# A routing map scattered into a DRAM scratch in place of a stage of one-hot matmuls, in a fused decoder layer

## The reference

```python
def peer_ffn(xn, w_q, sub_keys, u, v):
    q = (t @ w_q).reshape(T, PEER_HEADS, 2, PEER_HALF)
    s = jnp.einsum('thpd,hpnd->thpn', q, sub_keys)
    s_top, i_top = lax.top_k(s, PEER_TOPK)                       # 16 of 128, on each of two sides
    cand_s = s_top[:, :, 0, :, None] + s_top[:, :, 1, None, :]   # 256 candidates
    cand_i = i_top[:, :, 0, :, None] * PEER_KEYS + i_top[:, :, 1, None, :]
    best_s, pos = lax.top_k(cand_s, PEER_TOPK)
    ids = take_along_axis(cand_i, pos)                           # 8 heads x 16 experts for each token
    gates = jax.nn.softmax(best_s, axis=-1)
    act = gelu(einsum('td,ted->te', x, u[ids]))
    y = einsum('te,ted->td', gates * act, v[ids])
```

## Time and profile before

| | |
|---|---|
| median of 3 runs | 1158.25 us (1155.82 to 1158.5) |
| profiled execution, first to last instruction (span) | 1152.3 us |
| PE busy | 1085.2 us, 94% of the span |
| DVE busy | 786.0 us, 68% |
| ACT busy | 621.2 us, 54% |
| POOL busy | 120.7 us, 10% |
| moved by DMA | 179.54 MB, mean 156 GB/s |
| granted TensorE clock, mean | 0.980 |

### The profile page before, as it was taken

One profiled execution on the slowest core, in us unless ns is written; L12 is line 12 of the kernel. 1 busy time (PEld: TensorE's weight loads), 2 busy tenths in 40 slices (PEclk: granted clock), 3 DMA queues, 4 the chain that ended last, 5 costly groups with the idle time before them and its releaser, 6 DMA issues.

```text
span 1152.3 us, 20363 instructions
## 1 busy us (share of the span) xinstructions
PE 1085.2 (94%) x7278; PEld 1002.3 (87%) x7278; DVE 786.0 (68%) x1333; ACT 621.2 (54%) x1034; POOL 120.7 (10%) x101
## 2 busy tenths in 40 slices
PE   7999999989999999999999976667999999999998
PEld 6988999889899999999999975656888888888886
DVE  5774674453488889888884489998555555555554
ACT  6775555453555555555555576665545545455453
POOL 0000110010000000000000067884000000000000
PEclk9999999999999999999999988898999999999999
DMA  9544345252355454555445520001555555555552
GB/s 318 167 149 145 111 167 163 74 183 110 112 181 184 180 184 180 182 184 182 183 180 185 185 86 0 0 0 36 188 204 191 185 198 200 182 191 207 184 187 105
DMA packets 60658, 179.54 MB, mean 156 GB/s; under 512 B 4048, under 2 KB 42960, under 8 KB 44112
## 3 DMA queue, kind: packets, MB, share of 16 engines
q1 hardware_dynamic: 60624, 179.09, 44.7%
HBM read 178.03 MB, written 1.05 MB: 155 GB/s over the span
## 4 chain that ended last, share of the span: by engine, by line
PE 48%; issue 40%; DVE 7%; ACT 2%; POOL 2%; DMA 1%; DVEq 0%; POOLq 0%; SPq 0%; ACTq 0%
PE acc L1262 30%; PE acc L1044 13%; PE bank L1243 2%; DVE act_w L968 2%; DVE oh_i L957 2%; DVE oh_j L957 1%; POOL oh_i L320 1%; ACT wsp L347 1%; DVE wsp L663 1%; DMA wraw<-w_in 1%; PE bank L1148 0%; PE bank L1126 0%; POOL sqd L327 0%; PE bank L1073 0%; POOL wsp L312 0%
## 5 line engine op out<-in xcount | busy, mean ns | idle before, releaser
L886 DVE TENSOR_TENSOR hl<-raw,hl 128x1024 fp32r<-128x1024 f32 x192 | 234.4, 1225 | 170.0 <-ACT hl L577 168.2
L577 ACT ACTIVATE hl<-raw 128x1024 fp32r<-128x1024 f32 x192 | 202.6, 1056 | 135.7 <-PE acc L1262 126.3
L1262 PE MATMUL acc<-hl,whl 128*128 128x512 f32 x1152 | 266.6, 389 | 1.8 <-DVE whl L985 1.8
L1262 PEld LDWEIGHTS acc<-hl,whl 128*128 128x128 f32 x1152 | 216.3, 188 | 46.6 <-issue 1.9
L1214 PE MATMUL bank<-xt,hl 128*128 128x256 f32 x768 | 218.1, 284 | 0.0
L1215 PE MATMUL bank<-xt,hl 128*128 128x256 f32 x768 | 217.5, 283 | 0.0
L1216 PE MATMUL bank<-xt,hl 128*128 128x256 f32 x768 | 217.5, 283 | 0.0
L1214 PEld LDWEIGHTS bank<-xt,hl 128*128 128x128 f32 x768 | 147.5, 192 | 0.3 <-DVE hl L886 0.3
L1215 PEld LDWEIGHTS bank<-xt,hl 128*128 128x128 f32 x768 | 147.6, 192 | 0.2 <-issue 0.2
L1216 PEld LDWEIGHTS bank<-xt,hl 128*128 128x128 f32 x768 | 147.5, 192 | 0.0
L663 DVE TENSOR_TENSOR wsp<-wraw,wsp 128x2048 fp32r<-128x2048 f32 x35 | 80.2, 2290 | 73.9 <-ACT wsp L347 73.7
(11 more groups left out here) (207 smaller groups left out, 1448.3 us busy)
## 6 DMA issues: line engine op xcount, KB each, us to landing
raw<-u_t SPq DMA_DIRECT2D x64, 1024.0 KB, 4.8
raw<-v SPq DMA_DIRECT2D x64, 1024.0 KB, 4.7
wraw<-w_in SPq DMA_DIRECT2D x9, 1024.0 KB, 8.0
wraw<-w_pq SPq DMA_DIRECT2D x8, 1024.0 KB, 5.2
wraw<-w_ck SPq DMA_DIRECT2D x4, 1024.0 KB, 5.0
wraw<-w_cv SPq DMA_DIRECT2D x4, 1024.0 KB, 4.9
wraw<-w_out SPq DMA_DIRECT2D x4, 1024.0 KB, 4.9
wraw<-w_cq SPq DMA_DIRECT2D x4, 1024.0 KB, 5.0
```

The source lines that it names most:

```text
L577: nc.scalar.activation(eslot(k, 0, second), raw[:, k // 2, k % 2], ACT.Copy).then_inc(ready, 1)
L886: V.tensor_tensor(eslot(k, 1, second), raw[:, k // 2, k % 2], eslot(k, 0, second).bitcast(F32), ALU.subtract).then_inc(ready, 1)
L1262: last = pe.matmul(acc[:, 2 * t + n], a, b[:, 512 * n:512 * n + 512], start=False, stop=last_key and k == 2, skip_group_check=True)
```

## The change

The routing stage is gone. In its place W stands as an array `wmap` of 128 x 128 x 256 floats (16.8 MB) in DRAM:
- SP fills it with zeros in 8 transfers of 2.1 MB between the weight units 10 to 24 (new L260), from a tile of zeros that POOL clears at the start.
- Each routing pass ends with 16 addresses for each of its 128 tokens (`widx`), and its gates are normalised by themselves, two and four keys later: ACT's Exp (new L618) and two small instructions of DVE (new L917, L918).
- POOL then issues 16 indirect transfers for the pass (new L342), each of which adds one float per token to `wmap`: 256 transfers of 128 floats in all. Before a pass it waits until the pass of the previous head on the same tokens has landed.
- When all have landed, SP loads `wmap` for two keys at a time (256 KB, new L277 and L285) behind each load of v, and POOL multiplies it into act_w (`weigh`, new L348), 64 times. ACT splits a key of act_w only after that.
- ACT's loop over the keys is written out, and PE no longer transposes krow.

```diff
@@ SP
             for u in range(WRAW, NU):
                 unit(u)
+                if u % 2 == 0 and u // 2 - U_CK // 2 in range(NZERO):
+                    z = (u - U_CK) // 2
+                    n = KEYS * T // 512 // NZERO
+                    sp.dma_start(wz[:, z * n:z * n + n], zeros[:].unsqueeze(1).broadcast_to([P, n, 512])).then_inc(s_zero, 16)
...
             for q in range(2):
                 sp.wait_ge(s_ul, KEYS - 4 + 2 * q + 2)
                 sp.dma_start(raw[:, q], vd[q]).then_inc(s_raw[q], 16)
+            for t in range(TT):
+                sp.wait_ge(s_sca[t], 16 * TOPK * PH)
+            for q in range(2):
+                sp.dma_start(wblk[:, q], wm[:, WBK * q:WBK * q + WBK]).then_inc(s_wb[q], 16)
             sp.wait_ge(s_um, KEYS)
             sp.dma_start(gfin[:], g_final.rearrange("(o d) -> o d", o=1).broadcast_to([P, D])).then_inc(s_gf, 16)
             with sp.Fori(1, KEYS // 4) as it:
                 for q in range(2):
                     sp.wait_ge(s_vl, it * 4 - 4 + 2 * q + 2)
                     sp.dma_start(raw[:, q], vd[ds(it * 2 + q, 1)].rearrange("o i j d -> (o i) j d")).then_inc(s_raw[q], 16)
+                    sp.wait_ge(s_A, it * 2 + q - 1)
+                    sp.dma_start(wblk[:, q], wm[:, ds(it * (2 * WBK) + WBK * q, WBK)]).then_inc(s_wb[q], 16)
@@ POOL
-            (gate_rows, differences and their loop)
+            pool.wait_ge(s_zero, 16 * NZERO)
+            for n in range(NPASS):
+                t, h = n % TT, n // TT
+                pool.wait_ge(s_gr, n + 1)
+                if h:
+                    pool.wait_ge(s_sca[t], 16 * TOPK * h)
+                for k in range(TOPK):
+                    nc.gpsimd.indirect_dma_start(
+                        out=wmap, out_offset=bass.IndirectOffsetOnAxis(ap=widx[:, n, k:k + 1], axis=0),
+                        in_=gate[:, n, k:k + 1], in_offset=None, compute_op=ALU.add).then_inc(s_sca[t], 16)
+            def weigh(b, q):
+                aw = act_w[:, ds(b * WBK, WBK)]
+                nc.gpsimd.tensor_tensor(aw, aw, wblk[:, q], ALU.mult).then_inc(s_A, 1)
+            for b in range(2):
+                pool.wait_ge(s_ua, WBK * b + WBK)
+                pool.wait_ge(s_wb[b], 16)
+                weigh(b, b)
+            pool.wait_ge(s_ua, KEYS)
+            with pool.Fori(1, NWB // 2) as it:
+                for q in range(2):
+                    pool.wait_ge(s_wb[q], it * 16 + 16)
+                    weigh(it * 2 + q, q)
@@ ACT
+                if exps < NPASS and j == pass_key(exps) + 2:
+                    g = gate[:, exps]
+                    act.wait_ge(s_rt, exps + 1)
+                    nc.scalar.activation(g, g, ACT.Exp, accum_out=stat[:, GS + exps:GS + exps + 1]).then_inc(s_ge, 1)
+                    exps += 1
...
             for k in range(4):
+                if k % WBK == 0:
+                    act.wait_ge(s_A, k // WBK + 1)
                 a_high(k, k)
@@ DVE
+                if normed < NPASS and j == pass_key(normed) + 4:
+                    gate_norm(normed)
+                    normed += 1
+                if parts < 4 * NPASS and j == part_key(parts):
+                    route_part(parts // 4, parts % 4)
...
-            (onehots, weigh and their loop)
```

More of the change, by code:

```diff
@@ L19 @@
 X = mybir.AxisListType.X
+XY = mybir.AxisListType.XY
 ds = bass.ds
@@ L55, with build @@
 DVE_EVAC = set(range(U_OUT, U_CV3)) | set(range(U_CO, U_PQ))
-JPB = 8
-GRP = 4
-def build(nc, x, mem, par, wa, wx, w, keys_t, u_t, v, g_final, out):
+NPASS = TT * PH
+NZERO = 8
+WBK = 2
+NWB = KEYS // WBK
+def build(nc, x, mem, par, wa, wx, w, keys_t, u_t, v, g_final, wmap, out):
     ctx = ExitStack()
@@ L293, in _ @@
             nc.gpsimd.memset(ones[:], 1.0).then_inc(s_const, 1)
+            for t in range(TT):
+                nc.gpsimd.iota(tcol[:, t:t + 1], pattern=[[1, 1]], base=P * t, channel_multiplier=1,
+                               allow_small_or_imprecise_dtypes=True).then_inc(s_const, 1)
             nc.gpsimd.memset(cx[:, :, 0:CONV - 1], 0.0).then_inc(s_const, 1)
@@ L585, in _ @@
                 split_high(k, 16 if k % 2 == 0 else None, (s_seed, 1) if k == 2 else None, s_uh)
[L586 to L607, removed]
@@ L610, in onehots @@
[L610 to L618, removed]
-                last.then_inc(s_sqd, 1)
-                act.wait_ge(s_sqd, n + 1)
-                nc.scalar.activation(oh_j(slot), sqd(slot), ACT.Relu, scale=-1.0, bias=ones[:, 0:1]).then_inc(s_oja, 1)
@@ L623, in _ @@
-            act.wait_ge(s_kte, 3)
-            for slot in range(3):
-                onehots(0, slot, slot, GRP * slot, slot, True)
-            with act.Fori(1, T // GRP // 4) as it:
-                for slot in range(3):
-                    onehots(it, it * 3 + slot, it * 4 + slot, it * (4 * GRP) + GRP * slot, slot, False)
+            exps = 0
+            for j in range(KEYS):
+                gelu(j, j)
+                n = (j + 4) // 2
+                if j < KEYS - 4:
+                    split_high(j % 4, 16 * (n // 2 + 1) if j % 2 == 0 else None, (s_um, j + 1), s_uh)
+                elif j < KEYS - 1:
+                    split_high(j % 4, 16 * (n // 2 + 1) if j % 2 == 0 else None, (s_um, j + 1), s_vh, second=True)
+                if exps < NPASS and j == pass_key(exps) + 2:
[3 more added lines that the diff above has]
+                    exps += 1
@@ L1216, in u_keys @@
                         last = pe.matmul(bank[k][:, 0:T], ul[:, c], xt[:, c, 0], start=False, stop=(c == DC - 1))
-                    if last_pass and k < 3:
-                        if k == 0:
-                            pe.wait_ge(s_gr, 1)
-                        for t in range(TT):
-                            last = pe.transpose(bank[k][:, T + P * t:T + P * t + P], krow[:, k, t], ident[:])
                     last.then_inc(s_um, 1)
             u_keys(0, first=True)
-            with pe.Fori(1, KEYS // 4 - 1) as it:
+            with pe.Fori(1, KEYS // 4) as it:
                 u_keys(it)
-            u_keys(KEYS // 4 - 1, last_pass=True)
-            pe.wait_ge(s_ua, KEYS)
-            pe.wait_ge(s_kte, 3)
-            def route(it, slot, first=False):
-                pe.wait_ge(s_gi, it * 4 + (slot + 1))
-                if slot == 3:
-                    pe.wait_ge(s_ojd, it + 1)
-                else:
-                    pe.wait_ge(s_oja, it * 3 + (slot + 1))
-                if not first:
-                    pe.wait_ge(s_gw, it * 4 + (slot - 3))
-                for k in range(GRP):
-                    last = pe.matmul(bank[slot][:, P * k:P * k + P], oh_i(slot)[:, k], oh_j(slot)[:, k], start=True, stop=True)
-                last.then_inc(s_gm, 1)
-            for slot in range(4):
-                route(0, slot, first=True)
-            with pe.Fori(1, T // GRP // 4) as it:
-                for slot in range(4):
-                    route(it, slot)
             def v_wait(j):
```

184 lines of the change are left out of this document (67 added, 117 removed).

## The result

| | before | after |
|---|---|---|
| median | 1158.38 us (4 runs, 1155.82 to 1159.26) | 1223.61 us (4 runs, 1221.51 to 1224.97) |
| ratio after / before | | 1.0567 [1.0551, 1.0583] |
| span of the profiled execution | 1152.3 us | 1222.3 us |
| granted TensorE clock, mean | 0.980 | 0.912 |

The change makes the kernel 5.7% slower. The forecast was 1066 us, on the other side of no change. The time lies inside the range. The spans differ by more than the medians do, 70.0 us against 65.2. In every other run the time is 2.0 us above its span, as in 1224.35 and 1222.3 here, so the profiled execution of before was one of some 1154.3 us, about 4 us quicker than the median of its kernel.

The account below looks back on a forecast made before the run. PE was taken to bound the key and value stages, DVE the routing stage between. Span 1152.3 - 95.8 + 4 = 1060.5 us, plus 5.95 for the median, gave 1066 us; range 1034 to 1250.

Parts of the forecast that it names:

- What bounds the kernel, what goes: Key and value stages bound by PE, routing by DVE; removing routing starts the value stage at 673.8, gaining 124.4 us.
- The later of 673.8 and 344.0 + 256 X: Start of the value stage: everything else ready at 673.8, or POOL's 256 transfers plus a 6.6 us tail.
- the term X: Time POOL takes for each of 256 indirect transfers, chosen as 1.4 us; value start 702.4, gain 95.8 us.
- the 1.77 from which nothing is left: Time per POOL transfer, in us, at which the value stage starts at 798.2 as before, leaving no gain.
- the rival in which POOL is held until the landing: POOL waits for each transfer to land, 2.1 us each: value start 881.6, time 1246 us; chance 0.27.
- the forecast's own range: Whole kernel with 1.0 to 1.7 us per transfer and small losses: 1034 to 1144 us; chance 0.50.
- DVE's hold: Rival: DVE's two-input operations hold up POOL's transfers, 0.45 us each; value start 817.6, time 1182 us; chance 0.08.
- The start of 856 us: Value stage start if POOL were held for the skill's 2.0 us fixed per transfer: slower by 58 us.
- The DMA engines as the bound: Rival: small additions delay loads of u, the key stage grows by 54 us, time 1092 us; chance 0.06.
- a cost of the zeros: Filling the map between weight units 10 and 24: 2 us taken, up to 34 us if writes ran at half speed.
- The small losses: Zeros 2 us, Exp 0, DVE's key stage 0, key-stage traffic 1 us, value stage 1 us: 4 us in all.
- three signs of being wrong: Transfer spacing outside 1.0 to 1.7 us, PE waiting inside the key stage, ACT's value-stage waits naming POOL.

Follow-up runs that it names:

- experiment 3: The changed kernel with only the first 8 of the 16 transfers of each pass: 1031.23 us, ratio 0.8925.
- experiment 1: The changed kernel with its 256 indirect transfers as plain writes, without addition: 1075.01 us.
- experiment 4: The changed kernel with DVE's low splits of the key stage, from the fifth key on, cut from 1024 to 16 columns: 1183.37 us, ratio 1.0237.
- experiments 2 and 6: The changed kernel with each transfer cut from 128 to 64 partitions, with addition (1178.23 us) and as plain writes without addition (1066.35 us).
- experiment 7: The changed kernel with transfers for tokens 0 to 127 only (128 of them), the earlier one-hot routing stage for the other tokens: 1090.81 us, ratio 0.9437.

## Why the prediction was wrong

**What bounds the kernel, what goes:** right. The piece taken out was the 127.8 us of the routing stage, and a value stage with everything ready starts at 673.0 (experiment 3; predicted 673.8).

**The form of the new wait:** right. "The later of 673.8 and 344.0 + 256 X" gives 862.7 with the measured spacing, against 865.4. The missing 2.7 us are 2.4 for a first issue at 339.8 in place of 337.4 and 0.8 for a tail of 865.4 - 858.0 = 7.4 us in place of 6.6, less 0.5 because 256 X counts a gap and a hold behind the last transfer.

**The step that failed is the term X**, the time from one indirect transfer of POOL to the next, chosen as 1.4 us from POOL's arithmetic rows. It measured 2.026:

| part of X | us | from |
|---|---|---|
| a plain transfer of 128 floats | 0.96 | experiment 1 |
| the addition | 0.58 | experiment 1 |
| gap to the next ("issue") | 0.30 | timeline of after |
| mean hold by DVE's splits | 0.18 | 2.026 - 1.845; experiment 4 removes most of it |

Of the 0.626 us that were missing, the gap makes 0.31, the hold 0.18 and the duration 0.14. The gap between two transfers was not in the choice at all: the duration alone, 1.54, would still have given a gain, 1.54 + 0.305 gives none. The hold was put into a rival although the rows of before showed its like the earlier trace rows. That 1.4 came as near as it did to the duration of 1.54 is luck. The rows of arithmetic over 128 partitions were no guide to it: the price of a transfer hardly depends on the number of its rows (experiments 2 and 6), and 0.58 of it are the addition's. Without any hold X would be 1.845, past the 1.77 from which nothing is left, and experiment 4 with its 1.882 is slower than before. The sum with the measured value: 0.626 times 256 is 160 us, against 865.4 - 702.4 = 163 us by which the start was missed. The time still lies inside the range because the range was stretched to 1250 for the rival in which POOL is held until the landing, and that mechanism was not there: the hit is luck.

Two smaller slips of the sum: of the 5.95 us added to the span, only 2.0 lie outside it in every other run, the rest being a quick profiled execution; and the forecast's own range ends at 1143, not 1144.

**The rivals.** POOL held until the landing is refuted: the last issue ends at 857.98 and SP's load of the map, which waits for the landing, is only issued at 859.6, while in the stream the next transfer begins 0.30 us after the last. Nor does its "reads before it writes" hold POOL (experiment 3). The time of this rival was nearest in size, 1246 us, by a mechanism that was not there. DVE's hold was real and of another size: 0.18 in the mean where 0.45 was assumed, since only 156 of the transfers run beside the splits, and not each of them starts within one. The X of 1.85 in that rival is by chance the price of a quiet transfer with its gap. The Trainium skill, "SBUF — State Buffer", § Who interferes with whom, says that when a two-input Vector operation and a GpSimd instruction that reads SBUF overlap, the second to issue blocks until the first ends; the trace agrees for the transfers that start second (1.54 becomes 2.58). It does not for the splits: 78 of them start inside a transfer, and none takes longer than 1.24 us. The same section of the Trainium skill says that tensor_tensor did not stall transfers in a probe. Here one does stall an indirect transfer, and the measurement decides. The Trainium skill's price in "DMA: Bandwidth & Descriptors", § Latency and other measured facts, is about 1 us for the first byte, which it lays to emission by the issuer. That is near the 0.96 us of a plain transfer, and has neither the gap nor the addition in it: even without addition the spacing is 1.444, and the passes do not keep pace (1.16). The same page of the Trainium skill, § Anatomy of one DMA, gives about 2.0 us fixed for setup and completion of one transfer. The start of 856 us that was worked out from it comes nearest of all to 865.4, and by luck, for the 2.026 are made of other parts, as the table shows.

The DMA engines as the bound are refuted (PE's key stage is full), and so is a cost of the zeros: PE is busy for 114.1 us of the window 52 to 170.

**The small losses.** Exp with its table loads, the parts of the passes on DVE, and the traffic in the key stage cost nothing that the windows show: 368.9 us against 369.8. It starts 1.5 us and ends 0.8 us later, which is the most that can be laid to the zeros. In the value stage the product of POOL stays hidden from PE, but not by much: ACT waits for it 61 times, 24.9 us in all, and PE never.

```profile
ACT whl L622 <- POOL act_w L348: 24.9, 61, 0.6
```

So two of the three signs of being wrong came true, a spacing outside 1.0 to 1.7 us and ACT's waits that name POOL, and the second of them cost nothing. The value stage is 2.8 us longer all the same, for another reason (below). Experiment 3 bounds all of them together: span 1029.9, of which the value stage from 673.0 takes 356.9.

## What to carry to other kernels

Before work is moved to many small indirect transfers, multiply their number by the whole spacing from one issue to the next, about 1.85 us with addition and 1.27 without in a quiet stretch here, and compare it with the stretch that is to hide them; here 156 of 256 fitted. The number of transfers counts, not their rows, so few transfers of 128 rows are cheaper than twice as many of 64. If a stream is too long for its cover, split the work: the half that fits gave 5.6%, where the whole cost 5.7%.

## What the hardware showed that was not expected

- **The price of an indirect transfer is nearly fixed.** With addition it takes 1.54 us of POOL at 128 rows and 1.41 at 64, without it 0.96 and 0.89. The 0.58 us of the addition pass on POOL while no packet of an indirect transfer is under way (experiment 3), so they are not a wait for the DMA engines; what POOL does in them stays open.
- **An accumulating transfer makes 144 packets where a plain one makes 32,** and takes 7.8% of the engines' time against 0.5%, for the same 0.15 MB. It stayed harmless beside the loads of u.
- **The hold goes one way, and the order of start decides it.** A transfer that starts within a split of DVE waits for what is left of its 1.23 us (1.54 becomes up to 2.58). A split that starts within a transfer is not held (at most 1.24 us in 78 cases), and neither is the transfer.
- **Two streams can lock.** 18 transfers in a row started some 0.06 us behind the start of a split, because a hold makes the next start late by just the time between two splits. So the loss by holds is not the mean over random starts.
- **The hole costs a little more than its length.** The granted clock was 0.51 over the hole, so the lower level of 1.2 GHz, after PE had idled in it. The windows behind it:

```profile
865.40:867.00 1.60, 1.58 (x4) 1.31 (x5) 0.88 (x3) 0.35 (x2) 0.00 (x0) 0.50 1.00 404
...
871.00:873.00 2.00, 2.00 (x9) 1.62 (x9) 0.99 (x1) 1.40 (x2) 0.89 (x1) 0.91 0.48 176
```

For some 6 us the value matmuls run at half clock, up to 0.76 us each for 0.39, so about 3 us are lost. That accounts for the 2.8 us of the value stage. In experiment 3 PE idled for only 3.1 us, and its first 4 us were at 0.50 too, with a value stage of 356.9 us as here; in experiment 7, where matmuls ran at a clock of 0.95 ahead of it, it took 354.2, as before (354.1). So this part of the loss came with a pause of 3 us as with one of 194.
